# A recurrence's older products as one set, its GpSimd order, and where six dense products stand

## The reference

```python
def _rwkv7_scan(r, w, k, v, a, b):
    def step(state, inp):
        r_t, w_t, k_t, v_t, a_t, b_t = inp
        sa = jnp.einsum('bhvk,bhk->bhv', state, a_t)
        state = (state * w_t[:, :, None, :] + sa[..., None] * b_t[:, :, None, :]
                 + v_t[..., None] * k_t[:, :, None, :])
        return state, jnp.einsum('bhvk,bhk->bhv', state, r_t)
```

## Time and profile before

| | us |
|---|---|
| median of 3 runs | 1754.0 (1753.24 to 1755.06) |
| the profiled execution | 1754.57 |
| its span | 1752.8 |
| TensorE busy | 1654.6 |
| VectorE busy | 764.3 |
| ScalarE busy | 561.3 |
| GpSimd busy | 452.3 |
| mean granted clock of TensorE (1 is full speed) | 0.986 |

### The profile page before, as it was taken

One profiled execution on the slowest core, in us unless ns is written; L12 is line 12 of the kernel. 1 busy time (PEld: TensorE's weight loads), 2 busy tenths in 40 slices (PEclk: granted clock), 3 DMA queues, 4 the chain that ended last, 5 costly groups with the idle time before them and its releaser, 6 DMA issues. The chain is left out here.

```text
span 1752.8 us, 35509 instructions
## 1 busy us (share of the span) xinstructions
PE 1654.6 (94%) x15497; PEld 863.8 (49%) x15690; DVE 764.3 (44%) x1045; ACT 561.3 (32%) x883; POOL 452.3 (26%) x236
## 2 busy tenths in 40 slices
PE   4998889899999998899999999999999999999997
PEld 2455666666644555444444345444444444444443
DVE  5696555556425555312210388331323323222328
ACT  5323444444324555321212256321212112121200
POOL 2221322222110112022422123551423233232310
PEclk9999999999999999999999999999999999999999
DMA  9851001000101200411210211330202020212002
GB/s 358 285 175 32 15 6 38 4 27 27 28 25 49 61 1 1 137 44 36 72 36 24 96 49 37 103 129 21 85 20 76 24 72 26 70 36 84 1 0 97
DMA packets 105777, 109.75 MB, mean 63 GB/s; under 512 B 2592, under 2 KB 82610, under 8 KB 105394
## 3 DMA queue, kind: packets, MB, share of 16 engines
q1 hardware_dynamic: 105648, 107.82, 19.0%
HBM read 101.52 MB, written 4.19 MB: 60 GB/s over the span
## 5 line engine op out<-in xcount | busy, mean ns | idle before, releaser
L218 PE MATMUL tokens_ps<-a_hi,z 128*128 128x512 bf16 x878 | 228.5, 379 | 0.9
L674 PE MATMUL ff_ps<-ff_hi,c_lo 128*128 128x512 bf16 x503 | 190.6, 379 | 0.6
L674 PE MATMUL ff_ps<-ff_hi,c_hi 128*128 128x512 bf16 x501 | 189.9, 379 | 1.3 <-DVE z L2582 0.9
L674 PE MATMUL ff_ps<-ff_lo,c_hi 128*128 128x512 bf16 x501 | 189.9, 379 | 0.6
L2582 DVE TENSOR_TENSOR z<-ff_ps,z 128x512 f32<-128x512 f32 x128 | 88.3, 690 | 205.1 <-PE ff_ps L674 204.4
L2478 ACT ACTIVATE ff_r<-tokens_ps,cols 128x1024 f32<-128x1024 f32 x30 | 33.4, 1113 | 421.4 <-PE tokens_ps L218 414.4
L2404 POOL TENSOR_TENSOR z<-z 128x1024 bf16<-128x1024 f32 x28 | 62.1, 2219 | 345.5 <-ACT z L2400 345.5
L218 PEld LDWEIGHTS tokens_ps<-a_hi,z 128*128 128x128 bf16 x896 | 87.7, 98 | 105.7
L2570 DVE TENSOR_TENSOR ff_r<-ff_r 128x1024 f32<-128x1024 f32 x32 | 41.1, 1284 | 219.4 <-ACT ff_r L2478 219.4
L218 PE MATMUL tokens_ps<-a_lo,z 128*128 128x512 bf16 x438 | 131.1, 379 | 0.5
L195 POOL TENSOR_TENSOR mg_wlo<-mg_stage,mg_whi 128x1024 bf16<-128x1024 f32 x21 | 45.7, 2178 | 158.2 <-ACT mg_whi L191 158.2
(11 more groups left out here) (395 smaller groups left out, 3114.2 us busy)
## 6 DMA issues: line engine op xcount, KB each, us to landing
ff_st<-w_ff SPq DMA_DIRECT2D x8, 2048.0 KB, 7.7
z<-w_ff SPq DMA_DIRECT2D x30, 512.0 KB, 4.0
ada_w<-w_ada SPq DMA_DIRECT2D x6, 2048.0 KB, 8.3
z<-w_in SPq DMA_DIRECT2D x18, 512.0 KB, 4.9
z<-w_ada SPq DMA_DIRECT2D x8, 1024.0 KB, 13.4
mg_stage<-w_in SPq DMA_DIRECT2D x16, 512.0 KB, 3.9
zs_stage<-w_in SPq DMA_DIRECT2D x8, 512.0 KB, 7.3
ada_w<-w_ada SPq DMA_DIRECT2D x4, 1024.0 KB, 13.5
```

Source lines behind the costliest of these rows:

```text
L218: last = pe.matmul(out[:, h * HALF:(h + 1) * HALF], w[:, kt, :], a[:, slot, h * HALF:(h + 1) * HALF], start=(x == 0 and y == 0), stop=(x = ...
L674: last = pe.matmul(out, a[:, slot, at], w[:, x, n], start=(x == 0 and y == 0), stop=(x == k - 1 and y == 2))
```

## The change

M0 becomes one loop like that of M2: 16 products of 128 columns, b against both readers. NTd's rows of the lower 32 tokens now hold their diagonal block in columns 32 to 63, so two VectorE operations select it: one multiplies columns 32 to 63 by a mask of the lower rows into X, the other multiplies columns 0 to 31 by a mask of the upper rows and adds X. The dense products 6 to 11 of a turn, which stood behind the answer terms, stand in two groups of three, ahead of and behind the state terms. On GpSimd, dense_low(t + 2) is ahead of low(t - 3). Two reads of BAB are rewritten for the new layout.

```diff
             for t in range(TURNS):
                 if inside(t + 1):
                     front(t + 1)
+                dense_low(t + 2)
                 if inside(t - 3):
                     low(t - 3)
-                dense_low(t + 2)
...
                 for e in range(2):
-                    dve.tensor_tensor(NTd[:, 4 * e:4 * e + 4, :], half4(BAB[e], 0), of_head(t, e, CH), ALU.mult).then_inc(s["NTd"], 1)
+                    dve.tensor_tensor(NTd[:, 4 * e:4 * e + 4, :], q4(BAB[e])[:, :, 0:CH], of_head(t, e, CH), ALU.mult).then_inc(s["NTd"], 1)
                 wait(dve, t, "NTd")
+                dve.tensor_scalar(X[:], NTd[:, :, B:CH], g.misc(6), None, ALU.mult).then_inc(s["nd"], 1)
+                wait(dve, t, "nd", 1)
+                dve.scalar_tensor_tensor(NTd[:, :, 0:B], NTd[:, :, 0:B], g.misc(5), X[:], ALU.mult, ALU.add).then_inc(s["nd"], 1)
+                wait(dve, t, "nd")
...
-                    dve.tensor_tensor(W[f][:, 4 * e:4 * e + 4, 0, :], half4(BAB[e], 1), over(incl, NT), ALU.mult).then_inc(s["M1e"], 1)
+                    dve.tensor_tensor(W[f][:, 4 * e:4 * e + 4, 0, :], q4(BAB[e])[:, :, CH:P], over(incl, NT), ALU.mult).then_inc(s["M1e"], 1)
...
                         for e in range(2):
-                            pe.matmul(BAB[e][rows2[c2], (4 + j) * CH:(5 + j) * CH], bt[heads[e], at:at + CH], ar[f][heads[e], 1, at:at + CH],
-                                      start=True, stop=True)
-                for j in range(NT):
-                    for q in range(4):
-                        at, h = (2 * j + q // 2) * CH, q % 2
-                        for e in range(2):
-                            reads = ar[f][heads[e], 0, at:at + CH].rearrange("p (x n) -> p x n", x=2)
-                            if h:
-                                reads = ar[f][heads[e], 0, at + B:at + CH].unsqueeze(1).to_broadcast([HD, 2, B])
-                            last = pe.matmul(BAB[e][quads[q], j * CH:(j + 1) * CH].rearrange("p (x n) -> p x n", x=2),
-                                             bt[heads[e], at + h * B:at + h * B + B], reads, start=True, stop=True)
+                            last = pe.matmul(BAB[e][rows2[c2], j * P:(j + 1) * P].rearrange("p (x n) -> p x n", x=2), bt[heads[e], at:at + CH],
+                                             ar[f][heads[e], :, at:at + CH], start=True, stop=True)
                 last.then_inc(s["M0"], 1)
                 queries_maps(l)
+                if t:
+                    dense(2 * n, 6, 9)
                 state_terms(l)
+                if t:
+                    dense(2 * n, 9, 12)
                 answer_terms(l)
-                if t:
-                    dense(2 * n, 6, 12)
-                else:
+                if t == 0:
                     dense(1, 0, 16)
```

More of the change, by code:

```diff
@@ L984, in phase_recurrence @@
         BAB, BCD, HY = (BA, BB), (BC, BD), (HY0, HY1)
-        per_turn = {"M1e": 2, "NTd": 2, "NTm": 2, "PQa": NT, "M2e": 2, "TTm": 2, "T12e": 2, "ze": 2, "ge": 2, "ysb": 2, "PQ": 2, "TTe": 4, "Te": 5, "X": 4, "Xe": 4, "TX": 4,
+        per_turn = {"nd": 2, "M1e": 2, "NTd": 2, "NTm": 2, "PQa": NT, "M2e": 2, "TTm": 2, "T12e": 2, "ze": 2, "ge": 2, "ysb": 2, "PQ": 2, "TTe": 4, "Te": 5, "X": 4, "Xe": 4, "TX": 4,
                     "ch": NC, "S": NC}
-        names = ("gs du draw dz dhi dlo vs vz vdif vcopy kkr sq lw sg la a cum cumE eN eE eI t k2 aN ss ssm rn AT RT BT KT wc rk BhT KhT M0 pp TT0 M1e NTd NTm TTe Te "
+        names = ("nd gs du draw dz dhi dlo vs vz vdif vcopy kkr sq lw sg la a cum cumE eN eE eI t k2 aN ss ssm rn AT RT BT KT wc rk BhT KhT M0 pp TT0 M1e NTd NTm TTe Te "
                  "M2 M2e X Xe TX X21 X21e TTm T12 T12e vnT vne knT kne bnT bne anT ane mv mve PQ PQa PQd ZG ze ge HY S0 ch S out ysb cen yc sqy "
```

## The result

The changed kernel takes 1744.4 us against 1754.3, ratio 0.9943 (95% interval 0.9926 to 0.996): about 10 us faster, where 6 were predicted. A second measurement of it, beside 17 runs of the kernel before, gave 0.9932 (0.9919 to 0.9945).

What follows compares the result with a forecast made beforehand. TensorE, busy 1654.6 of 1752.8 us, was taken as the bound; -4.5 - 2.9 + 1.3 + 0.3 - 2.0 + 1.7 = -6.1 us gave 1748.5 from 1754.57 and 1747.9 from the median 1754.0, predicted 1748, range 1740.5 to 1754.

Steps and rivals of the forecast that it cites:

- rival (a): Recurrence: moved dense products before each fast group end the instruction stalls, up to -9.1 us more; 1739 to 1745, chance 0.22.
- The wait for GpSimd, -4.5: Start of turns 4, 5 and 6: TensorE's waits for GpSimd's cut of the dense weights go, -4.5 us in all.
- The PQ copy: ScalarE's copy that the older products wait for: next late, but covered by six dense products of 1.3 us.
- The products, -0.48 a turn: M0 in turns 1 to 6: one set takes 0.93 us instead of 1.41, -2.9 us in all.
- The seam, +0.21 a turn: Turns 1 to 6: one more return from small float32 products to dense ones, +1.3 us in all.
- The pair: VectorE's two added operations: 0.88 us, covered in turns 1 to 6 by 1.3 us of slack; +0.3 in turn 7.
- The half clock, -2.0: Start of turns 5 and 6: full clock once the GpSimd wait goes, about 1.0 us a turn, -2.0.
- the stalls in its place, +1.7: Turns 5 and 6: at full clock, issue stalls come, about +1.0 us a turn less the present 0.34.
- The stalls of turns 1 to 4, 0: Two block crossings a turn, 0.3 to 0.7 and 1.2 to 1.5 us, again about 1.8 a turn: no change.
- the mean crossing that makes the kernel no faster: Slower case, answer terms and correction back to back: slower once the mean crossing costs over 1.4 us; 1758, chance 0.05.
- half-block weight: TensorE's instruction stream: a block crossing's cost weighed by what TensorE does in the half block before it, 0.65 to 1.2 us.
- theory A: From the experiments: about 256 TensorE instructions cannot be used up in under some 3.3 us; the shortfall is an issue stall.

Runs made afterwards that it cites:

- the table: Kernels with GpSimd's order, moved products and one set alone, in pairs and all together, plus repeats; ratios to the kernel before from 0.9926 to 1.0005.
- the kernel with the shifted grid: Changed kernel plus 32 tiny bf16 products (64 TensorE instructions with loads) ahead of the recurrence's first dense unit; one execution took 1740.6 us.

## Why the prediction was right, and where it was not

The range held the time and the direction was right, but the sum said 6.1 where 14 to 15 were gained in the recurrence and 10 to 12 in the time. The 1744.4 us lie outside the forecast's own band of 1745 to 1750.5 and in that of rival (a), 1739 to 1745, which had a chance of 0.22. The range is right because it took this rival in. By its steps:

- **The wait for GpSimd, -4.5: right.** The waits are gone, and putting them back costs 4.5 us in turns 0 to 6. The PQ copy, named as next late, did not come up.
- **The products, -0.48 a turn: right.** 0.43 net with the seam.
- **The seam, +0.21 a turn: too high.** About 0.05.
- **The pair: its price was right (0.88 against 0.90), its cover wrong.** The step listed the correction's waits for X and gt, and stopped at gt. Behind gt on ScalarE stood the table load and the root, and the logits wait for the root's read: 0.62 us in turns 5 and 6. In turn 7 the chain for X costs 1.02 instead of 0.75, and gt 0.67: TensorE has the copy of X 7.94 us after its M0 instead of 7.41, +0.5 where +0.3 was written.
- **The half clock, -2.0, and the stalls in its place, +1.7.** In the changed kernel the clock is full there, and no issue stall stands in turns 5 and 6 (the root's waits do). The 2.0 was about right: of the 12.9 us gained in turns 0 to 6, 4.5 of waits, 2.6 of products and 5.2 of stalls, less 1.2 of root waits, leave 1.8 for it. But it was partly a matter of which trace was read, since the half clock does not come behind every wait. The trade exists, as the kernel with GpSimd's order alone shows, but the second half of it did not fall due here.
- **The stalls of turns 1 to 4, 0: this is the term that failed.** The places were right, the first crossing in the state products and the second in the correction. The costs were not: 0.65 on average for the crossing in the correction, where 1.2 to 1.5 were written, and nothing over 0.2 for the first crossing, where 0.3 to 0.7 were. Turns 1 to 4 have 2.8 us (2.4 in the second trace) instead of 7.4, and turns 1 to 6, with none in the last two, the same 2.8 instead of 9.4. The prediction had named this as a sign of being wrong, an issue total far from 9 us. Rival (a) gave the right direction, with the wrong agent: it credited the moved products. The one set did it: with it the stalls are 2.3 to 3.0 us in every kernel of the table, moved products or not, and without it 6.2 to 10.4.

Three figures of the prediction do not come out of its own numbers, without changing the forecast: no stalls at all would be -9.4 and not -9.1 against its count; the mean crossing that makes the kernel no faster is (9.4 + 6.1) / 12 = 1.3 us and not 1.4; and the "1.8 us a turn" of its signs holds for turns 1 to 4 alone, as the sum has 1.0 in turns 5 and 6.

The Trainium skill ("Runtime: NRT & Kernel Launch", Instruction fetch mechanics) also says that an engine fetches "the next page while executing the current one". The grid of 256 agrees with its block, and packets that start 1.1 to 1.9 us after TensorE has entered a block agree with the fetch beside the work; the stalls of 0.2 to 2.2 us at single crossings do not agree with its "mostly hidden".

The half-block weight of the prediction fails on the kernel with the shifted grid. A least time per block (theory A) holds for a block entered out of a stall, with 3.4 to 4.1 us instead of a fixed 3.3, and not for others. What stays open is the size of the first stall of a row: what starts a packet when TensorE has not just been stopped was not measured.

That the one set makes the stalls smaller is shown by four pairs of kernels. Two rivals come with it. It also moves the grid, and the kernel with the shifted grid shows that this alone changes the stalls. In turns 1 and 3 this rival is out: 128 (t + 1) is there a whole number of blocks, so the boundaries fall on the same products as before (27 and 20 matmuls of the correction are left behind the stall in both kernels), and yet the first stalls, 0.59 and 0.72, are gone; without the moved products nothing over 0.2 us is left there at all. In turns 2 and 4 the two are not separated. And the set never ran without VectorE's pair; TensorE does not wait for VectorE or for gt in turns 1 to 4 of the changed kernel, but a run of the pair alone is missing.

## What to carry to other kernels

Where small float32 products follow each other, count their instructions beside their time: a stall marked issue that returns every 250 instructions or so, and ends soon after a packet of the instruction queue has landed (1.2 to 1.6 us here), is the stream being fetched, and fewer, wider products paid twice here. When an operation is added to an engine that seems idle, follow what is queued behind the receiver on the next engine, to the end, not only to the first wait. And put an operation that needs a late input behind one that others wait for.

## What the runs showed of the hardware

A stall of TensorE marked issue stood on the same instruction in two traces of one kernel and moved with the count of instructions ahead of it: 613 to 486 in turn 3, by 3 x 128 and whole blocks of 256. It ended 1.20 to 1.63 us after a 16 KB packet of the instruction queue had landed, in all 141 cases of turns 1 to 7. Its size varied between executions, 1.23, 1.50 and 1.78 us for the same boundary in three traces that share the stretch around it, as the packet came sooner or later. At half clock the same boundaries of turns 5 and 6 were cheap or did not show (0.34 us in the kernel before), and at full clock they did (0.76 and 0.55 in the kernel with GpSimd's order alone, 1.00 and 0.41 in turn 6 of the kernel before's second trace). A half-clock stretch fell on 6 of the 15 starts of turns 4 to 6 behind a wait of TensorE for GpSimd of 1.1 to 1.5 us, and on none of the 27 without it.
